# Hymba-style encoder block on one core: state-space products for both directions at once, log dt in the exponent, and a new order of convolution, projections and mLSTM products

## The reference, cut to what matters

```python
acum = jnp.cumsum(dt * A.reshape(G, hg), axis=2)
xdt = x * dt[..., None]
seg = acum[:, :, :, None] - acum[:, :, None, :]
decay_ts = jnp.exp(jnp.where(tril[:, :, None, None], seg, -jnp.inf))
cb = jnp.einsum('bctgn,bcsgn->bctsg', Cm, Bm)
y_diag = jnp.einsum('bctsgh,bcsghp->bctghp', cb[..., None] * decay_ts, xdt)
...
y_f = _ssd_chunked(xs, dt[..., :H], A[:H], Bm, Cm)
y_b = fl(_ssd_chunked(fl(xs), fl(dt[..., H:]), A[H:], fl(Bm), fl(Cm)))
y = y_f + y_b + d_skip.astype(jnp.float32)[:, None] * xs
```

## Time and profile before

| | |
|---|---|
| device time, median of 3 runs | 744.17 us (743.95 to 746.29) |
| span of the profiled execution | 744.0 us |
| the profiled execution's own time | its span; 0.2 us under the median of the runs |
| PE busy | 713.8 us, 96% |
| DVE, ACT, POOL busy | 260.9, 165.0, 48.0 us |
| input projection, scores and scans | to 210 us |
| output projection | 213 to 269 us |
| norm and router | 259 to 288 us |
| experts | to 733 us, transfers at 420 to 430 GB/s |

### The profile page before, as it was taken

The page is one execution under the profiler, slowest core; times in us unless marked ns, Lnnn a source line. Parts: engine busy times, 40 slices in busy tenths (PEclk is TensorE's granted clock), DMA queues, the critical chain, the costliest instruction groups (busy, mean ns, idle before and its releaser), DMA issues.

```text
span 744.0 us, 11161 instructions
## 1 busy us (share of the span) xinstructions
PE 713.8 (96%) x4514; PEld 416.7 (56%) x4518; DVE 260.9 (35%) x639; ACT 165.0 (22%) x345; POOL 48.0 (6%) x65
## 2 busy tenths in 40 slices
PE   7999999999999999999999999999998999999993
PEld 6888888888864455445444435444443445444441
DVE  3401599657757085222112211022211122112225
ACT  1010423407940043111111111111111121111111
POOL 0120020320320020100000000000000000000000
PEclk9999999999999999999999999999999999999997
DMA  8964544544398548999999999999999999999993
GB/s 335 406 209 142 177 164 169 179 161 165 119 385 364 226 173 344 357 370 425 424 420 430 424 430 432 427 428 422 432 427 427 425 426 423 425 424 424 418 404 134
DMA packets 30946, 251.01 MB, mean 337 GB/s; under 512 B 4000, under 2 KB 4800, under 8 KB 10032
## 3 DMA queue, kind: packets, MB, share of 16 engines
q1 hardware_dynamic: 27792, 240.78, 79.4%
q0 software_dynamic: 2448, 8.48, 3.2%
q10 hardware_dynamic: 656, 1.05, 0.4%
HBM read 249.31 MB, written 1.11 MB: 337 GB/s over the span
## 4 chain that ended last, share of the span: by engine, by line
PE 72%; DMA 10%; DVE 9%; SPq 6%; issue 1%; ACT 1%; DVEq 0%
PE bank L1212 20%; PE bank L820 16%; DMA arena<-in_we_dram 10%; PE bank L1280 8%; PE bank L963 7%; PE bank L1131 7%; DVE arena L1603 5%; PE bank L1149 4%; SPq L627 3%; PE bank L934 1%; PE bank L900 1%; SPq L636 1%; PE bank L1254 1%; PE bank L1289 1%; ACT bank L1368 1%
## 5 line engine op out<-in xcount | busy, mean ns | idle before, releaser
L1212 PE MATMUL bank<-arena 128*64 128x512 f32 (+2 forms) x1008 | 198.8, 601 | 5.4 <-DMA arena<-in_we_dram 5.4
L820 PE MATMUL bank<-arena 128*128 128x256 f32 x768 | 167.7, 379 | 0.0
L820 PEld LDWEIGHTS bank<-arena 128*128 128x128 f32 x768 | 145.6, 190 | 20.5 <-issue 0.4
L1212 PEld LDWEIGHTS bank<-arena 128*64 128x64 f32 (+2 forms) x1008 | 57.7, 127 | 96.6 <-issue 94.0
L1280 PE MATMUL bank<-arena 128*64 128x512 f32 (+2 forms) x512 | 91.7, 584 | 3.5 <-DMA arena<-in_we_dram 2.1
L1131 PEld LDWEIGHTS bank<-onehotb,h_part 128*128 128x128 bf16 x1200 | 67.2, 98 | 19.4 <-issue 19.4
L1131 PE MATMUL bank<-onehotb,h_part 128*128 128x128 bf16 x1200 | 71.3, 219 | 0.0
L1928 DVE TENSOR_TENSOR y_lo<-bank,y_hi 128x512 fp32r<-128x512 f32 (+1 forms) x51 | 34.7, 681 | 101.9 <-ACT y_hi L1513 75.5
L1905 DVE TENSOR_REDUCE arena<-bank 64x1 f32<-64x3 f32 (+1 forms) x64 | 10.1, 158 | 160.8 <-PE bank L1230 160.2
L1280 PEld LDWEIGHTS bank<-arena 128*64 128x64 f32 (+1 forms) x512 | 26.3, 124 | 54.0 <-issue 44.6
L963 PE MATMUL bank<-arena 128*128 128x512 f32 x128 | 55.3, 592 | 0.0
(11 more groups left out here) (276 smaller groups left out, 493.6 us busy)
## 6 DMA issues: line engine op xcount, KB each, us to landing
arena<-in_we_dram SPq DMA_DIRECT2D x82, 1024.0 KB, 19.6
arena<-in_we_dram SPq DMA_DIRECT2D x17, 3072.0 KB, 30.8
arena<-in_we_dram SPq DMA_DIRECT2D x22, 2048.0 KB, 31.4
arena<-in_wc_dram SPq DMA_DIRECT2D x15, 1024.0 KB, 11.2
arena<-in_wn_dram SPq DMA_DIRECT2D x8, 1024.0 KB, 4.7
arena<-in_wo_dram SPq DMA_DIRECT2D x8, 1024.0 KB, 4.8
apart<-in_we_dram SPq DMA_DIRECT2D x7, 1024.0 KB, 29.7
arena<-decay_rows POOLq DMA_DIRECT2D x5, 1024.0 KB, 7.1
```

What stands on the lines that cost most here:

```text
L820: mm = nc.tensor.matmul(bank[n % 2][:, j * S:(j + 1) * S], wk, xk, start=(k == 0), stop=(k == KD - 1))
L1212: mm = nc.tensor.matmul(bank[0][rows[q], :], hc[v][:, k, rows[q]], place[at_q[part][q]][:, c:c + 512], start=(k == 0), stop=(k == KD - 1))
```

## The change

- **log dt.** DVE clamps dt at 1e-37, ACT takes its logarithm (one ACTIVATE after unit 2, `log_dt`), and DVE adds it to the column terms of the exponents. The decay factor of a state-space block then contains dt, so x needs no multiplication by dt: `dt_x`, `dt_col` and two of the eight gate-column transposes go.
- **One product for both directions.** Inside a chunk, the forward and backward blocks can now be added before they meet the scores and x. DVE does per family two sums and four multiplications in place of six multiplications. PE does per group 8 products of 128x256 (64 columns of weights) in place of 8 of that size and 8 of 128x128.
- **Where the exponentials go.** Of six blocks of a state-space family, two are written straight to the weight tiles, four to banks 2 and 3.
- **Order.** Eight of the 16 convolution tiles stand ahead of the copies of the mLSTM scores. The state-space scores and transposes of x stand after unit 14 and not after unit 16. The mLSTM products of a token half stand together, with one unit ahead of each half; the units 19 to 24 stand ahead of the four state-space groups. The squares stand after step 3 of the output projection, not after step 1.

The diff, cut to its core:

```diff
+EARLY_CONV = 8
-SQUARES_AFTER = 1
+SQUARES_AFTER = 3
...
-        ZROWS = ((ZSTEP, ZSTEP + 1), (ZSTEP + 2,), (ZSTEP + 3,), ())
+        AHEAD_OF = ((OSTEP + 2,), (OSTEP + 3,), (ZSTEP, ZSTEP + 1), (ZSTEP + 2, ZSTEP + 3))
...
-            sp.wait_ge(ssm_ready, 4)
-            load_first(13)
             sp.wait_ge(decay_exp, FAMS * NB)
             load_first(15)
             sp.wait_ge(y_ready, 1)
             load_first(16)
             load_first(19)
+            sp.wait_ge(ssm_ready, 4)
+            load_first(13)
...
-            for n in range(VSTEP, OSTEP):
+            for n in range(VSTEP, VSTEP + 2):
                 project_unit(n)
...
+            for n in range(VSTEP + 2, OSTEP):
+                project_unit(n)
             n = 0
             for t in range(T):
+                project_unit(OSTEP + t)
                 for hd in range(H):
-                    if hd % 2 == 0:
-                        z = 2 * t + hd // 2
-                        project_unit(OSTEP + z)
...
+                    for s in range(T):
                         for i in range(2):
                             j = 2 * c + i
+                            to = ps[i * HP:(i + 1) * HP, :].rearrange("p (u t) -> p u t", u=T)
                             col = (4 * g + j) * HP
-                            mm = nc.tensor.matmul(to, xdt[:, d, s, col:col + HP], mv_w, start=first, stop=last,
-                                                  skip_group_check=True)
+                            mm = nc.tensor.matmul(to, xs[:, s, col:col + HP], both[s][:, :, j, :], start=(s == 0),
+                                                  stop=(s == T - 1), skip_group_check=True)
...
+            act.wait_ge(dt_ready, 1)
+            nc.scalar.activation(g_log, g_dt, ACT.Ln).then_inc(log_dt, 1)
...
             decay_exps(3, 2, NB)
+            z_copy(0)
+            z_copy(1)
+            decay_exps(4)
             z_copy(2)
-            decay_exps(4)
             z_copy(3)
...
+            link(V.scalar_tensor_tensor(out=col_d, in0=g_log, scalar=rc[:, 6:7], in1=col_d, op0=ALU.mult, op1=ALU.add))
...
+                for t in range(T):
+                    m = weights_upto(fam - 1) + 2 * t
+                    w = W[fam % 2][5 if t else 0]
+                    dve.wait_ge(decay_exp, fam * NB + 3 * t + 2)
+                    V.tensor_tensor(w, exp_bank(m), w, ALU.add).then_inc(weight_ready, 1)
+                    gate_between(between, 2 * t)
+                    dve.wait_ge(weight_ready, m + 1)
+                    link(V.tensor_tensor(w, w, scores(t, t), ALU.mult))
+                    dve.wait_ge(decay_exp, fam * NB + 3 * t + 3)
+                    V.tensor_tensor(W[fam % 2][4 if t else 1], exp_bank(m + 1), scores(t, 1 - t), ALU.mult
+                                    ).then_inc(weight_ready, 1)
...
             dve.wait_ge(s_conv, 32)
+            for c in range(EARLY_CONV):
+                dve.wait_ge(proj_evac, CPAIR + 4 + c // 2)
+                conv(c)
             for hd in range(H):
                 misc_copy(M_ST + hd, st[:, hd, :, :], mbank(M_ST + hd, 2))
             dve.wait_ge(misc_evac, M_ST + H)
-            weights(0)
-            for c in range(CT):
+            ml_weights()
+            for c in range(EARLY_CONV, CT):
```

More of the change, by code:

```diff
@@ L199, in build @@
         g_z, g_nz, g_u, g_w, g_r, g_s, g_s2, g_p, g_sp, g_dec, g_cum, g_x, g_it, g_m, g_tr, g_zero = tmp
+        g_dt, g_log = [at(O_W + (16 + i) * S, S, rows=R) for i in range(2)]
         wgi = at(O_HML, KD, 2 * R)
@@ L841, in _ @@
                     ps = misc(M_COL)
[L842 to L845, removed]
+                    for t in range(T):
+                        mm = nc.tensor.transpose(ps[:, t * R:(t + 1) * R], g_tr[:, t * P:(t + 1) * P], ident[0:R, 0:R])
                     mm.then_inc(misc_ready, 1)
@@ L1354, in decay_exps @@
             def decay_exps(fam, first=0, end=NB):
-                for b, (d, s, t, diag) in list(enumerate(BLOCKS))[first:end]:
-                    n = fam * NB + b
+                for at_n, b in list(enumerate(SSM_ORDER if fam else range(NB)))[first:end]:
+                    d, s, t, diag = BLOCKS[b]
+                    n = fam * NB + at_n
                     act.wait_ge(rows_masked, 4 * fam + MASKED_AT[b])
@@ L1359, in decay_exps @@
                         act.wait_ge(misc_evac, M_COL2 + 1)
[L1360 to L1361 removed]
+                    if fam == 0:
+                        used, to = n, exp_bank(n)
+                    elif at_n in SSM_BANKED:
+                        used = weights_upto(fam - 1) + SSM_BANKED.index(at_n)
+                        to = exp_bank(used)
+                    else:
+                        used, to = 0, W[fam % 2][5 if at_n else 0]
+                        if at_n == 0 and fam == 2:
+                            act.wait_ge(ml_ready, 16)
+                        elif at_n == 0 and fam > 2:
+                            act.wait_ge(ssm_ready, fam - 2)
+                    if used >= 2:
+                        act.wait_ge(weight_ready, used - 1)
                     for j in range(4):
[L1363 removed]
                         hd = SH + j if fam == 0 else 4 * (fam - 1) + j
@@ L1367, in decay_exps @@
                             row = masked[ROWS_AT[fam]][:, d, j, :]
-                        ex = nc.scalar.activation(ps, row, ACT.Exp,
+                        ex = nc.scalar.activation(to[:, j, :], row, ACT.Exp,
                                                   bias=colT[:, (0 if diag else 4) + 2 * s + d, hd:hd + 1])
@@ L1385, in conv_act, with v_copy, o_gate, z_copy @@
                                      ACT.Silu).then_inc(conv_silu, 1)
+            def v_copy(n):
+                evac(n, vext[:, :, n - VSTEP, 0:DV], pair(n))
+            def o_gate(n):
+                evac(n, osig[:, :, (n - OSTEP) * S:(n - OSTEP + 1) * S], pair(n), func=ACT.Sigmoid)
+            def z_copy(i):
+                evac(ZSTEP + i, zT[:, 2 * i:2 * i + 2, :], pair(ZSTEP + i))
             for m in range(4):
                 conv_act(m)
[L1389 to L1396, removed]
-            def z_copy(i):
-                evac(ZSTEP + i, zT[:, 2 * i:2 * i + 2, :], pair(ZSTEP + i))
+            v_copy(VSTEP)
+            for m in range(4, 8):
+                conv_act(m)
+            v_copy(VSTEP + 1)
+            decay_exps(1)
+            v_copy(VSTEP + 2)
+            v_copy(VSTEP + 3)
+            o_gate(OSTEP)
+            o_gate(OSTEP + 1)
             decay_exps(2)
-            z_copy(0)
             decay_exps(3, 0, 2)
+            o_gate(OSTEP + 2)
+            o_gate(OSTEP + 3)
             act.wait_ge(var_ready, 1)
             nc.scalar.activation(vv[:, 1, 0:8], vv[:, 0, 0:8], ACT.Sqrt).then_inc(sqrt_done, 1)
-            z_copy(1)
             act.wait_ge(norm_ready, 1)
@@ L1608, in conv, with gate_between, ml_weights @@
                 ins.then_inc(conv_done, 1)
+            def gate_between(between, at_n):
+                if at_n < len(between):
+                    other, c = between[at_n]
+                    v = hml[:, c // 2, c % 2 * 512:(c % 2 + 1) * 512]
+                    dve.wait_ge(ml_normed, 2 * c + 2)
+                    o = other(c)
+                    link(V.tensor_tensor(v, v, o, ALU.mult))
+            def ml_weights():
+                for b, (d, s, t, _) in enumerate(BLOCKS):
+                    dve.wait_ge(decay_exp, b + 1)
+                    V.tensor_tensor(W[0][b], exp_bank(b), st[:, :, s, t * P:(t + 1) * P], ALU.mult).then_inc(weight_ready, 1)
             def weights(fam, between=()):
```

61 lines of the change are left out of this document (19 added, 42 removed).

## The result

| | before | changed |
|---|---|---|
| device time, median of 4 runs each | 745.09 us | 751.25 us |
| ratio, 95% interval | 1 | 1.0081 [1.0064, 1.0098] |
| span of the profiled execution | 744.0 us | 748.7 us |
| start of unit 1 of the projection | 10.55 us | 10.92 us |
| start of the output projection | 212.57 us | 219.36 us |

The sign was right. The time lies 0.95 us above the end of the range and 3.7 us above the forecast of 747.5 us.

What follows compares the result with a forecast made beforehand. PE was taken to set the pace up to the output projection, whose shift reaches the end. The terms -0.15 + 4.5 - 0.9 + 1.7 - 3.4 + 0.1 + 1.5 = +3.3 us on 744.2 gave 747.5 us, range 744.8 to 750.3.

Steps and rivals of the forecast that it cites:

- What bounds the kernel: PE sets the pace up to the output projection; a shift of that projection's start is worth itself at the end.
- Gate columns: At the gate-column transposes, two of eight go: -0.15 us; the logarithm on ACT was taken as 0.
- convolution ahead of the copies: At the mLSTM scores, head 2 waits for DVE's copy behind eight convolution tiles: +4.5 us, bounds 2.4 and 5.5.
- State-space scores and transposes: Before unit 17, PE no longer waits for DVE's convolution, so 7.4 us become 6.5 us: -0.9 us.
- mLSTM products: Eight results come together per half, so PE waits for DVE to read them: +1.7 us, between 1.0 and 2.5.
- State-space products: In the four groups, the eight short pairs go, priced by columns: -0.86 us per group, -3.4 us for four.
- second rival: State-space groups gain by instructions, not columns: they save 5.4 us, with low mLSTM waits sum +0.6, 744.8 us; chance 0.10.
- Weights in time: At the state-space groups, weights are ready before PE needs them, family 3 only closely: 0, up to 1 us if something slips.
- End of the scans: After group 3, the transposes wait for DVE's first copy of y, behind the products with z: +1.5 us.
- the clock: Rival: the clock falls in the new wait before head 2, costing 1.6 us: +4.9 us, 749.1 us; chance 0.30.
- Absorption: Rival: in the expert stage, transfers make up for the late start and hide all 3.3 us, 744.2 us; chance 0.06.
- the change gives what it is shaped for: Rival: at the score copies the 4.5 us term is gone: -1.2 us, 743.0 us; chance 0.05, of which 0.03 faster.

Runs made afterwards that it cites:

- e1: The changed kernel with six early convolution tiles ahead of the score copies in place of eight: 745.42 us, ratio 1.0001 to before.
- e3: The changed kernel with nine useless products on PE between the scores of heads 1 and 2, filling the wait: 750.04 us, ratio 1.0059 to before.
- e2: The changed kernel with seven early convolution tiles in place of eight: 747.77 us, ratio 1.0029 to before.
- e7: e1 with DVE's copies of y and last sum ahead of the products with z of groups 0 and 1: 744.08 us, ratio 0.9985 to before.
- e5: The new arithmetic alone on the order of the kernel before, no early convolution tile: 749.46 us, ratio 1.0067 to before.
- e6: e5 with six convolution tiles ahead of the score copies and squares after step 3: 749.50 us, ratio 1.0068 to before.
- e8: e6 with the copies of y ahead of the products with z: 749.72 us, ratio 1.0066 to before.
- e4: The kernel before with eight early convolution tiles and nothing else of the change: 751.55 us, ratio 1.0084 to before.
- e9: e6 with all six exponential blocks of family 3 behind the root and the normalising on ACT: 744.84 us, ratio 1.0002 to before.

## Why the prediction was wrong, point by point

**What bounds the kernel.** Right: the start of the projection carries the difference. In all eleven experiments the change in device time, by the ratio, follows that of the projection's start within 1.3 us.

**Gate columns, convolution ahead of the copies.** Right. The wait is 4.50 us against a term of 4.5 us; the transposes save 0.13 us.

**State-space scores and transposes.** Right: 6.5 us from 118.96 to 125.49.

**mLSTM products.** Right in mechanism, too small. The two halves take 152.50 - 146.21 = 6.3 and 6.35 us in place of 5.2 each: +2.2 us against +1.7. The view of waits shows 0.5 us twice; most of the loss is in gaps too short for it, and only the length of the block shows it.

**State-space products.** Right by columns: a group takes 1.88 us, 0.8 us less. The second rival is excluded.

**Weights in time.** PE did not wait for family 3, but with 0.06 us to spare where the prediction had 0.4 (193.8 against 194.2 us). With fewer early tiles or a filled wait it did wait: 0.43 us in e1, 0.18 in e3.

**End of the scans.** Right: from group 3's end to the projection 219.36 - 215.45 = 3.9 us against 2.5, +1.4 us for +1.5 forecast.

**The step that failed: the clock.** The prediction had it as a rival with 0.30, at 1.6 us, and made its sum without it. It happened, and cost 2.4 us. Two things were wrong. First the size: I took the one case of the trace, where 3.24 us of work fell in the low stretch; here 4.88 us did. Second the chance: I argued that one wait of 4.4 us need not do what the one of 3.2 us did, where the changed kernel shows it after 4.5 us and e2 after 2.1. The caution was not baseless: after 2.69 us in the expert stage of e1 and 3.2 us in that of e7 the granted clock stayed at 1.00. With 2.4 us for the clock and 2.2 for the products the sum would have been +6.2 us; the difference of medians is 6.2 and the projection came 6.4 us later. The Trainium skill, page "TensorE: Matmul & The Clock Gate", section "Part 1: The HAM clock gate (the 'warmup' mystery)", has the clock halved by idleness and given back by sustained work; e3 agrees, since the granted clock stayed at 1.00 when useless work filled the gap.

**The time that the sum is set on.** I put the span of 744.0 us at 0.2 us under the median and took them as one. In the later runs, the device time lies 1.8 to 2.9 us above the span, mostly 1.9, so the profiled execution of before was probably a slow one of its kind, near 745.9 us. The median of before was 744.17 us over three runs, 745.09 over four, and 744.3 to 745.6 over 22 or 23. The move of the median from 744.2 to 745.1 us accounts for 0.9 us of the 3.7 us by which the forecast fell short; the clock (2.4 us) and the mLSTM products (0.5 us) account for the rest.

**The range.** The 746.0 to 748.7 us that the prediction gives "by the bounds" is narrower than its bounds: added up they run from +0.6 to +5.1 us, 744.8 to 749.3 us. With the clock at its own 1.6 us on top, the upper end would have been 750.9 us and not 750.3; the measured time lies above that too.

**Absorption.** In the profile of the changed kernel, the stretch from the projection to the end is 529.3 us against 531.4. One wait for an expert transfer of 1.3 us is gone. I don't count it as absorption: with the projection as late as 217.5 to 218.4 us it is 530.9 to 531.6 us in e3, e5, e6 and e8, and the shortest, 528.5 us, is in e4. The medians show nothing of it. Why the transfers come sooner in some executions was not found.

**That the change gives what it is shaped for.** Half right: without the wait and the clock the other parts come out at +0.1 us (e1), since 2.2 us at the mLSTM products and 1.4 us at y eat what the groups (3.4 us) and the state-space scores give.

## What to carry to other kernels

When an instruction is moved ahead of a copy that another engine waits for, the question is not how long it takes but what its own inputs wait for: six tiles were free, the seventh and eighth brought the arrival of unit 8 into the path. On a kernel that PE bounds, price a new wait of PE with a fall of the clock behind it as well: in the scan stage here every wait from 2.1 to 5.6 us had one in the profile, and it cost 1.7 us (e2, e4) to 2.4 us (changed) on top of the wait. And a change of arithmetic changes where intermediate results live, and with that which queue blocks; count the destinations too.

## What the runs showed that I had not expected

- After a wait of PE of 2.1 us the granted clock fell to 0.50 for 3.41 us (e2), after 2.6 us for 3.41 us (e9), after 4.5 us for 6.83 us (changed) and 3.41 us (e4), after 5.6 us for 6.83 us (e5, e6, e8). After 1.7 us it stayed at 1.00 (changed, e1, e3). The same wait can give one or the other length; why was not found.
- In the expert stage a wait of 3.2 us lowered the clock in the kernel before and did not in e7. The wait ended at 565.53 us in the one and at 563.42 us in the other, so in e7 PE was busy for 1.94 us of the first stretch below, against 0.39 in the earlier trace rows. Whether that decided it was not tested:

```profile
561.95:565.36 3.41, 1.94 (x10) 0.92 (x12) 0.00 (x0) 0.00 (x0) 0.00 (x0) 1.00 0.93 399
565.36:568.77 3.41, 3.41 (x20) 1.26 (x18) 0.53 (x3) 0.00 (x0) 0.00 (x0) 1.00 1.03 440
```

- Nine products that compute nothing, put into the wait, bring PE to the output projection 2.2 us sooner (e3).
